# A product of 512 columns for the expert scores, with its halves added by ScalarE and VectorE

## The reference

```
q = x @ w_q                          # 256 x 2048: 8 heads, two halves of 128 each
s = q . sub_keys                     # 128 keys for each head and half
top_s, top_i = top_k(s, 16)          # 16 best keys of each half
best_s, best_c = top_k(sums of pairs, 16)        # 16 of 16 x 16 pairs
expert = i1 * 128 + i2               # one of 16384 experts, 128 per token
gates = softmax(best_s)
h = gelu(x . u_tab[expert])          # exact gelu
y = sum over experts of gates * h * v_tab[expert]
x = LayerNorm(alpha * x + y)
```

## Time and profile before

| | |
|---|---|
| median of three runs | 1952.9 us |
| the profiled execution | 1952.5 us |
| its span | 1950.7 us |
| mean granted TensorE clock | 0.992 |
| busy: TensorE (PE) | 1912.2 us, 98% |
| busy: VectorE (DVE) | 1421.8 us, 73% |
| busy: ScalarE (ACT) | 910.3 us, 47% |
| busy: GpSimd (POOL) | 363.8 us, 19% |
| U tiles of layer 0, first matmul to last | 190.8 to 586.0 us |
| V tiles of layer 0 end | near 966 us |

### The profile page before, as it was taken

One profiled execution on the slowest core, in us unless ns is written; L12 is line 12 of the kernel. 1 busy time (PEld: TensorE's weight loads), 2 busy tenths in 40 slices (PEclk: granted clock), 3 DMA queues, 4 the chain that ended last, 5 costly groups with the idle time before them and its releaser, 6 DMA issues.

```text
span 1950.7 us, 41638 instructions
## 1 busy us (share of the span) xinstructions
PE 1912.2 (98%) x14552; PEld 1713.1 (88%) x14552; DVE 1421.8 (73%) x2405; ACT 910.3 (47%) x1416; POOL 363.8 (19%) x266
## 2 busy tenths in 40 slices
PE   8989999999999999999999899999999999999998
PEld 7779999999998888888787799999999988888886
DVE  7978997577778888544588789975777788884445
ACT  6445454444444444444364454544444444444443
POOL 0000000000004444444300000000000044444443
PEclk9999999999999999999999999999999999999999
DMA  6244556554545455655452445565454545547553
GB/s 228 90 150 154 181 175 202 164 169 154 169 158 166 162 161 172 236 184 192 142 173 91 161 143 183 173 204 168 155 169 155 171 154 170 163 161 245 185 191 109
DMA packets 90502, 328.44 MB, mean 168 GB/s; under 512 B 10049, under 2 KB 10561, under 8 KB 90177
## 3 DMA queue, kind: packets, MB, share of 16 engines
q1 hardware_dynamic: 87264, 316.71, 50.0%
q10 hardware_dynamic: 3168, 10.89, 1.6%
HBM read 324.41 MB, written 3.15 MB: 168 GB/s over the span
## 4 chain that ended last, share of the span: by engine, by line
PE 91%; DVE 4%; issue 3%; ACT 1%; DMA 1%; DVEq 0%; POOL 0%; SPq 0%; ACTq 0%; POOLq 0%
PE bank L1140 15%; PE bank L1141 14%; PE bank L1142 14%; PE bank L1155 13%; PE bank L1157 13%; PE bank L1156 13%; PE bank L1377 5%; DVE conv_acc L734 1%; PE bank L1222 1%; PE bank L1347 1%; DVE lo L665 0%; DVE residual L699 0%; DVE small L689 0%; DMA raw<-in_stream 0%; PE bank L1266 0%
## 5 line engine op out<-in xcount | busy, mean ns | idle before, releaser
L665 DVE TENSOR_TENSOR lo<-raw,hi 128x1024 fp32r<-128x1024 f32 x600 | 766.1, 1279 | 262.5 <-ACT hi L402 260.7
L402 ACT ACTIVATE hi<-raw 128x1024 fp32r<-128x1024 f32 x600 | 634.1, 1059 | 465.9 <-PE bank L1157 439.9
L1140 PE MATMUL bank<-xt,hi 128*128 128x256 f32 x2432 | 696.9, 287 | 5.1 <-DVE xt L671 4.7
L1142 PE MATMUL bank<-xt,lo 128*128 128x256 f32 x2432 | 687.0, 282 | 0.0
L1141 PE MATMUL bank<-xt,hi 128*128 128x256 f32 x2432 | 686.9, 282 | 0.0
L380 POOL TENSOR_TENSOR w_split<-h,w_split 128x256 fp32r<-128x256 f32 x256 | 362.4, 1416 | 1569.4 <-ACT w_split L603 1179.3
L1140 PEld LDWEIGHTS bank<-xt,hi 128*128 128x128 f32 x2432 | 460.9, 190 | 9.7 <-DVE xt L671 4.3
L1141 PEld LDWEIGHTS bank<-xt,hi 128*128 128x128 f32 x2432 | 461.0, 190 | 0.0
L1142 PEld LDWEIGHTS bank<-xt,lo 128*128 128x128 f32 x2432 | 460.6, 189 | 0.0
L1155 PE MATMUL bank<-hi,w_split 128*128 128x512 f32 x1024 | 409.4, 400 | 0.6 <-POOL w_split L380 0.6
L1157 PE MATMUL bank<-hi,w_split 128*128 128x512 f32 x1024 | 404.4, 395 | 0.0
(11 more groups left out here) (165 smaller groups left out, 1070.4 us busy)
## 6 DMA issues: line engine op xcount, KB each, us to landing
raw<-in_stream SPq DMA_DIRECT2D x600, 512.0 KB, 3.7
ln_g<-in_ln_p ACTq DMA_DIRECT2D x4, 512.0 KB, 7.7
ln_b<-in_ln_p ACTq DMA_DIRECT2D x4, 512.0 KB, 9.7
keys_sb<-in_keys_t ACTq DMA_DIRECT2D x2, 1024.0 KB, 5.2
x_kept<-x ACTq DMA_DIRECT2D x4, 512.0 KB, 5.8
x<-x_kept ACTq DMA_DIRECT2D x4, 512.0 KB, 7.4
x<-in_x SPq DMA_DIRECT2D x2, 512.0 KB, 4.9
result<-x SPq DMA_DIRECT2D x4, 256.0 KB, 2.0
```

The costliest lines, as they stand in the source:

```text
L402: nc.scalar.activation(hi[:, j, :], raw[:, j, :], ACT.Copy).then_inc(*hi_done.one)
L665: vec.tensor_tensor(lo[:, j, :], raw[:, j, :], hi[:, j, :].bitcast(f32), ALU.subtract).then_inc(*lo_done[j].one)
L1140: mm(dst, w_hi, xt[:, k, 0, :], start=k == 0, stop=False)
L1142: last = mm(dst, w_lo, xt[:, k, 0, :], start=False, stop=k == KC - 1)
```

## The change

- A U tile is no longer computed by tile_by_x (which stays for AG and WQ tiles). The high weight is multiplied by both parts of x in one product of 512 columns: the lower half of the bank gets high by high, the upper half gets high by low. The low weight times the high x goes to the lower half in a product of 256 columns, as before. So there are 16 matmuls per tile instead of 24.
- ScalarE copies the upper half to h (u_half). VectorE adds the lower half of the bank to it, in place in h (add_halves, signal u_added). ScalarE then takes the gelu in place in h, three tiles late (GELU_LAG = 3).
- TensorE's reuse of a bank waits for u_added in place of gelu_done.
- On VectorE, each low part n from tile U4 on is followed at once by the add of tile n - 4 (ADD_LAG = 4), also between the steps of the choice. The lists of low parts are the same.
- The exponential of the gates moves on ScalarE from turn 8 to turn 9, and the transposes of the chosen keys from turn 11 to turn 13.
- The first gate_block of each segment waits for the last adds and gelus, which are written out ahead of it.

```diff
-EXP_TURN, CHOSEN_TURN = 8, 11
+EXP_TURN, CHOSEN_TURN = 9, 13
+ADD_LAG, GELU_LAG = RING, RING - 1
...
-        gelu_done = signal("gelu_done", NK, primed=RING)
+        u_half, u_added = signal("u_half_kept", NK), signal("u_added", NK, primed=RING)
+        gelu_done = signal("gelu_done", NK)
...
+                def gelu(i, j):
+                    act.wait_ge(*u_added(layer, RING * i + (j + 1)))
+                    act.sem_inc(act_held, 1)
+                    nc.scalar.activation(u_block(i, j), u_block(i, j), ACT.Gelu)\
+                      .then_inc(*gelu_done.one)
...
                         act.wait_ge(*tile_used(layer, RING * i + (U0 + j + 1)))
-                        nc.scalar.activation(h[:, ds(i * (RING * SEQ) + j * SEQ, SEQ)],
-                                             ring_banks[j][:, 0:SEQ], ACT.Gelu)\
-                          .then_inc(*gelu_done.one)
+                        nc.scalar.activation(u_block(i, j), ring_banks[j][:, SEQ:2 * SEQ],
+                                             ACT.Copy).then_inc(*u_half.one)
+                        if not first or j >= GELU_LAG:
+                            gelu(i, j - GELU_LAG)
...
+                def add_halves(i, j):
+                    dve.wait_ge(*u_half(layer, RING * i + (j + 1)))
+                    here = h[:, ds(i * (RING * SEQ) + j * SEQ, SEQ)]
+                    vec.tensor_tensor(here, ring_banks[j][:, 0:SEQ], here, ALU.add)\
+                       .then_inc(*u_added.one)
...
                     for n in range(made[0], made[0] + count):
                         rest(0, n)
+                        if n - ADD_LAG >= U0:
+                            add_halves((n - ADD_LAG - U0) // RING, n % RING)
...
                         for j in range(GROUP_TILES):
-                            rest(i + first_tile // RING, GROUP_TILES * k + j + LO_LEAD)
+                            if seg == 0:
+                                u_rest(i + G_TURN, GROUP_TILES * k + j, first and k == 0)
+                            else:
+                                rest(i + V0 // RING, GROUP_TILES * k + j + LO_LEAD)
...
+                for j in range(LO_LEAD, RING):
+                    add_halves(G_TURN - 1, j)
                 dve.wait_ge(*gelu_done(layer, SEG))
...
                 def u_tile(i, j, last_of_x=False):
                     pe.wait_ge(*lo_done[j](layer, i + (U0 // RING + 1)))
-
-                    pe.wait_ge(*gelu_done(layer, RING * i + (j - RING + 1)))
-                    tile_by_x(j, ring_banks[j][:, 0:SEQ], last_of_x)
+                    pe.wait_ge(*u_added(layer, RING * i + (j - RING + 1)))
+                    dst = ring_banks[j]
+                    for k in range(KC):
+                        w_hi, w_lo = hi[:, j, k * P:(k + 1) * P], lo[:, j, k * P:(k + 1) * P]
+                        both = xt[:, k, :, :].rearrange("p s t -> p (s t)")
+                        if k:
+                            mm(dst[:, 0:SEQ], w_lo, xt[:, k, 0, :], start=False, stop=False)
+                        last = mm(dst[:, :], w_hi, both, start=k == 0, stop=k == KC - 1)
+                        if k == 0:
+                            last = mm(dst[:, 0:SEQ], w_lo, xt[:, k, 0, :], start=False, stop=False)
```

More of the change, by code:

```diff
@@ L317, in build @@
         out_done = signal("out_done", 1, 16)
+        act_held = ctx.enter_context(nc.semaphore("act_held"))
         pe_held = ctx.enter_context(nc.semaphore("pe_held"))
@@ L391, in _ @@
             act.wait_ge(*consts_made(0, 1))
-            for _ in range(RING):
-                act.sem_inc(gelu_done.sem, 1)
             with act.Fori(0, DEPTH) as layer:
@@ L564, in _, with u_block, u_turn @@
                 nc.scalar.preload_act_table(ACT.Gelu)
-                def u_turn(i, before_last=None, after_first=None):
+                def u_block(i, j):
+                    return h[:, ds(i * (RING * SEQ) + j * SEQ, SEQ)]
+                def gelu(i, j):
[3 more added lines that the diff above has]
+                      .then_inc(*gelu_done.one)
+                def u_turn(i, before_last=None, after_first=None, first=False):
                     for j in range(RING):
@@ L573, in u_turn, with last_gelus @@
                         act.wait_ge(*tile_used(layer, RING * i + (U0 + j + 1)))
-                        nc.scalar.activation(h[:, ds(i * (RING * SEQ) + j * SEQ, SEQ)],
-                                             ring_banks[j][:, 0:SEQ], ACT.Gelu)\
-                          .then_inc(*gelu_done.one)
-                u_turn(0, after_first=lambda: score_group(SCORE_GROUPS - 1))
+                        nc.scalar.activation(u_block(i, j), ring_banks[j][:, SEQ:2 * SEQ],
+                                             ACT.Copy).then_inc(*u_half.one)
+                        if not first or j >= GELU_LAG:
+                            gelu(i, j - GELU_LAG)
+                def last_gelus(i):
+                    for j in range(RING - GELU_LAG, RING):
+                        gelu(i, j)
+                u_turn(0, after_first=lambda: score_group(SCORE_GROUPS - 1), first=True)
                 with act.Fori(1, EXP_TURN) as i:
@@ L586, in _ @@
                     u_turn(i)
+                last_gelus(G_TURN - 1)
                 act.wait_ge(*tables(layer, TT))
-                with act.Fori(G_TURN, LAST) as i:
+                u_turn(G_TURN, first=True)
+                with act.Fori(G_TURN + 1, LAST) as i:
                     u_turn(i)
@@ L606, in _ @@
                 u_turn(LAST, first_w_heads)
+                last_gelus(LAST)
                 def v_turn(i):
@@ L651, in _ @@
                 dve.sem_inc(w_done.sem, 1)
+            for _ in range(RING):
+                dve.sem_inc(u_added.sem, 1)
             vec.tensor_copy(ident_b[:, :], ident[:, :]).then_inc(*masks_made.one)
@@ L1031, in _, with u_rest @@
                 dve.sem_inc(dve_held, 1)
+                def u_rest(i, j, alone=False):
+                    rest(i + U0 // RING, j + LO_LEAD)
+                    if not alone:
+                        add_halves(i + (j + LO_LEAD) // RING - ADD_LAG // RING,
+                                   (j + LO_LEAD) % RING)
                 def u_rests(i):
                     for j in range(RING):
-                        rest(i + U0 // RING, j + LO_LEAD)
+                        u_rest(i, j)
                 with dve.Fori(CHOSEN_TURN + 1, G_TURN) as i:
@@ L1072, in gate_block, with gate_turn @@
                                       ALU.mult).then_inc(*w_done.one)
-                def gate_turn(seg, i, first_tile, following):
+                def gate_turn(seg, i, following, first=False):
                     for k in range(TURN_GROUPS):
@@ L1087, in _ @@
                 gated(0, 0, 0)
+                for j in range(LO_LEAD, RING):
+                    add_halves(G_TURN - 1, j)
                 dve.wait_ge(*gelu_done(layer, SEG))
                 dve.sem_inc(dve_held, 1)
-                with dve.Fori(0, G_TURN - 1) as i:
-                    gate_turn(0, i, U0 + NK // 2, (0, i + 1, 0))
-                gate_turn(0, G_TURN - 1, U0 + NK // 2, (1, 0, 0))
+                gate_turn(0, 0, (0, 1, 0), first=True)
+                with dve.Fori(1, G_TURN - 1) as i:
+                    gate_turn(0, i, (0, i + 1, 0))
+                gate_turn(0, G_TURN - 1, (1, 0, 0))
+                for j in range(LO_LEAD, RING):
+                    add_halves(LAST, j)
                 dve.wait_ge(*gelu_done(layer, NK))
@@ L1097, in _ @@
                 with dve.Fori(0, G_TURN - 1) as i:
-                    gate_turn(1, i, V0, (1, i + 1, 0))
-                gate_turn(1, G_TURN - 1, V0, None)
+                    gate_turn(1, i, (1, i + 1, 0))
+                gate_turn(1, G_TURN - 1, None)
                 with dve.Fori(G_TURN, LAST) as i:
@@ L1130, in transpose_x, with tile_by_x @@
                                 last.then_inc(*xt_ps.one)
-                def tile_by_x(slot, dst, last_of_x=False, xt_before=None):
+                def tile_by_x(slot, dst, xt_before=None):
                     for k in range(KC):
@@ L1142, in tile_by_x @@
                         last = mm(dst, w_lo, xt[:, k, 0, :], start=False, stop=k == KC - 1)
-                        if last_of_x and k == WHI_LEAD - 1:
-                            last.then_inc(*xt_used.one)
                     last.then_inc(*tile_used.one)
@@ L1364, in u_tile @@
                     pe.wait_ge(*lo_done[j](layer, i + (U0 // RING + 1)))
-                    pe.wait_ge(*gelu_done(layer, RING * i + (j - RING + 1)))
-                    tile_by_x(j, ring_banks[j][:, 0:SEQ], last_of_x)
+                    pe.wait_ge(*u_added(layer, RING * i + (j - RING + 1)))
[8 more added lines that the diff above has]
+                            last = mm(dst[:, 0:SEQ], w_lo, xt[:, k, 0, :], start=False, stop=False)
+                        if last_of_x and k == WHI_LEAD - 1:
+                            last.then_inc(*xt_used.one)
+                    last.then_inc(*tile_used.one)
```

(2 more changed lines are left out.)

## The result

The changed kernel takes 1971.1 us (median of 4 runs, 1970.3 to 1972.1), the kernel before 1954.6 us (median of 4, 1952.9 to 1958.3). The ratio is 1.008, with a 95% interval of 1.0068 to 1.0093: 0.8% slower, where 1970.0 was forecast. The profiled execution has a span of 1970.2 us, against 1950.7.

The account below looks back on a forecast made before the run. VectorE was taken to bound U4 to U39 of each layer. Over two layers, +24.5 us for the adds and -7.0 us for shorter tiles made +17.5 on 1952.5 us, so 1970.0 us, with a range of 1962 to 1979.

Parts of the forecast that it names:

- The bound: U4 to U39 of each layer: VectorE, busy 101.2 of 102.1 us, already sets the pace and TensorE waits for it.
- The loss: U4 to U39: 36 adds of 0.34 us on a full VectorE lengthen the stretch by 12.2 us per layer.
- The gain: U39 to the end of U127: 89 tiles each 0.039 us shorter on TensorE, -3.5 us per layer.
- The places without a cost: After the choice, beside the gate matrices and where they or the V tiles begin: adds are hidden, at zero cost.
- the same chain stands, and the same answer holds: Start of the V tiles: the wait for copy, add and last gelus is hidden as at the first gate matrices.
- the same chain at the first gate matrices: After U63: copy, add and last gelus end about 0.75 us later than the matmuls awaited before, hidden by 0.7 us.
- The turns: Exponential at turn 9, transposes at 13: they prevent a TensorE wait at the transposes and are priced at zero.

Follow-up runs that it names:

- e2: The kernel before with only the U tiles' matmuls changed (8 of 512, 8 of 256 columns), old gelu, no additions: 1945.7 us, ratio 0.9957.
- e1: The changed kernel without VectorE's additions for U0 to U53, all waits and signals kept: 1950.7 us, ratio 0.998.
- e6: The changed kernel with a second addition of the same form ahead of each of the first 38 additions: 1997.7 us, ratio 1.0216.
- e8: The changed kernel with the additions between the steps of the choice over only 128 of 256 columns: 1967.6 us.
- e7: e5 with the last four U tiles of each layer (U124 to U127) in the old form too: 1947.4 us, ratio 0.9961.
- e4: The changed kernel with the exponential and the transposes of the chosen keys back at turns 8 and 11: 1971.9 us, ratio 1.0085.
- e5b: The same kernel as e5, measured again beside e7 on one chip: 1952.0 us, ratio 0.9981.
- e5: The changed kernel with the old form for U0 to U43, the new from U44, exponential and transposes at turns 8 and 11: 1950.9 us, ratio 0.9979.
- e3: The changed kernel with 24 matmuls of 256 columns per U tile as before, copies, additions and lagged gelus kept: 1981.9 us, ratio 1.0138.

## Why the prediction was right

*The bound.* VectorE was said to set the pace from U4 to U39 in the kernel before, against a busy TensorE of 100%. e2 shows it (a third of the matmuls gone, 102.03 us all the same), and so the 73% of the page's mean was the wrong number to go by.

*The loss.* Forecast 36 x 0.34 = 12.2 us per layer, measured 11.66. The add costs 0.324 and not 0.34; e1, e6 and e8 give it by removal, by doubling and by half. It is the sum's largest term and was 5% too large. (The add behind U4's low part, 0.2 us per layer ahead of U4, was not in the sum.)

*The gain.* Forecast 0.039 us per tile, measured 0.044: 2.803 us per tile and 6.407 us per two tiles with gate matrices, against 2.809 and 6.41. For U39 to U127 this made -3.7 us per layer; -3.5 was forecast. 8 matmuls fewer (and their weight loads), at equal columns, are worth 5.5 ns each here. The Trainium skill's 6 cycles per matmul ("TensorE: Matmul & The Clock Gate", back-to-back issue gap), which it gives for the gap of an isolated matmul, would make 2.5 ns; the measurement decides for the larger one.

*The places without a cost.* It held after the choice, beside the gate matrices and where they begin (U66 starts 2.4 us after its low part). It failed at the start of the V tiles: "the same chain stands, and the same answer holds" was not worked out. This is the timeline of VectorE there in the changed kernel, with the operation of GpSimd and the gate matrices that matter.

```profile
597.10 0.69 DVE L1110 TENSOR_TENSOR h<-bank,h 128x512 f32 x1 [1.30 <-ACT h L575]
597.71 0.95 DVE L1085 TENSOR_TENSOR onehots<-key_blocks,i_t 128x1536 bf16<-128x1536 bf16 x1
598.58 1.77 DVE L688 TENSOR_TENSOR lo<-raw,hi 128x1024 fp32r<-128x1024 f32 x1
600.26 1.49 DVE L1095 TENSOR_TENSOR gated_a<-onehots,gate_part 128x1536 bf16<-128x1536 bf16 x1
...
600.18 0.76 POOL L383 TENSOR_TENSOR w_split<-h,w_split 128x256 fp32r<-128x256 f32 x1 [0.92 <-ACT w_split L616]
...
601.81 0.87 PE L1432 MATMUL bank<-gated_a,onehots 128*128 128x64 bf16 x24 [0.41 <-DVE gated_a L1095]
```

And the same operations in the kernel before:

```profile
587.00 0.69 DVE L1071 TENSOR_TENSOR h<-bank,h 128x512 f32 x1 [1.99 <-PE bank L1377]
587.61 0.95 DVE L1046 TENSOR_TENSOR onehots<-key_blocks,i_t 128x1536 bf16<-128x1536 bf16 x1
588.47 1.76 DVE L665 TENSOR_TENSOR lo<-raw,hi 128x1024 fp32r<-128x1024 f32 x1
590.16 0.94 DVE L1056 TENSOR_TENSOR gated_a<-onehots,gate_part 128x1536 bf16<-128x1536 bf16 x1
...
592.28 0.88 PE L1377 MATMUL bank<-gated_a,onehots 128*128 128x64 bf16 x24
```

Before, the factors are ready at 591.10, 1.18 us ahead of the gate matrices. After the change the gate block waits for the last gelu (line 575) and starts 5.13 us behind the start of U127 (591.97) instead of 3.96 (U127 at 583.04): 1.17 us later, where the prediction put 0.75 for the same chain at the first gate matrices. By these rows that alone would just have been covered. But so shifted, the gated factors run beside GpSimd's split of h and take 1.49 us instead of 0.94; TensorE waits 0.41 us and starts its gate matrices 9.84 us behind the start of U127 instead of 9.24. In all eleven traces this operation takes 1.48 to 1.50 us in just the 16 places where GpSimd's split overlaps it (by some 0.67 us), one in each layer of the eight that have this chain, and at most 0.96 us in the others, which none overlaps. In e7 the last U tiles are in the old form, the block doesn't wait for a gelu, and the same operations stand as before (U127 starts at 578.50):

```profile
582.46 0.69 DVE L1131 TENSOR_TENSOR h<-bank,h 128x512 f32 x1 [1.99 <-PE bank L1462]
...
585.62 0.94 DVE L1116 TENSOR_TENSOR gated_a<-onehots,gate_part 128x1536 bf16<-128x1536 bf16 x1
...
587.74 0.88 PE L1462 MATMUL bank<-gated_a,onehots 128*128 128x64 bf16 x24
```

That was 1.2 us in two layers, priced at zero; e7 shows that the chain causes it, and how it divides between the later block and the slower factors is read from these rows, not tested. *The turns* were priced at zero, and e4 confirms it; but the reason given, that they prevent a wait of TensorE, was wrong: at turn 11 there is none.

Over two layers the errors are 1.2 us too much for the loss, 0.4 too little for the gain and 1.2 left out at the V tiles; they nearly cancel. The forecast difference of 17.5 us stands against 17.1 in the four stretches, 16.5 between the medians and 19.5 between the spans of the two profiled executions. That the total lies 1.1 us from the forecast is in part luck; the terms are right to about 1.2 us each over two layers.

## What to carry to other kernels

Before giving an engine more work, look at its busy share in every stretch. Here VectorE was at 73% as a mean and at 99% for 102 us per layer, and 36 operations of 0.32 us in those 102 us cost more than 8 matmuls less in each of the 89 tiles behind them gave back. An engine that shows 100% busy is not yet the bound: compare its time per tile in the stretch with its time per tile elsewhere. And a gain that is real can be kept by using the new form only where the engine that pays has room: e7 takes the same change to 0.4% under before.

## What the runs showed of the hardware that was not expected

Runs of one kernel spread by 2 to 9 us (e5b 1946.0 to 1955.1), as much as the effects of e5 and e7. Part of it is TensorE's granted clock in the attention stage of each layer. The window of 94 to 104 us, in the kernel before and in e3, whose work up to U0 is the same:

```profile
94.00:104.00 10.00, 9.81 (x56) 7.04 (x57) 7.05 (x22) 8.36 (x25) 0.00 (x0) 1.00 0.44 145
```

```profile
94.00:104.00 10.00, 10.00 (x30) 7.02 (x30) 5.86 (x17) 5.68 (x15) 0.00 (x0) 0.50 0.18 65
```

The clock is at 2.4 GHz (1.00) in the one and at 1.2 GHz (0.50) in the other, for the same work; 56 matmuls fall in the one window and 30 in the other. Just ahead of it TensorE was idle for 1.9 us, waiting for ScalarE's copy of v, and it is so in all eleven traces, in both layers. What follows is not the same, even for one kernel (e5 and e5b). From the end of this idle time to U0 of layer 0:

| low clock behind the idle time, layer 0 | profiled execution of | us to U0 |
|---|---|---|
| none | before, after, e2, e5b, e7 | 96.5 to 96.7 |
| 3.4 us | e4, e5 | 98.1 to 98.2 |
| 10.2 us | e1, e3, e6, e8 | 101.2 to 101.4 |

So 10.2 us at the low clock cost 4.6 us here, and 3.4 us cost 1.5. In layer 1 the stretch at the low clock lasts 3.4 us in most of the traces, none in e5b, 6.8 us in e8 and 10.2 us in e1, and the way to U0 goes with it: 97.0 us in e5b, 98.1 to 98.6 in most, 100.3 in e8, 101.3 in e1. The executions of e1 agree: those of 1947 us have a mean granted clock of 0.992, those of 1954 to 1955 us one of 0.987. Which execution gets the low clock is not told apart by anything I could see in the traces before that point. It is not the whole spread either: the idle time itself ends between 93.2 us (e7) and 96.7 us (e8).

The second is the add's price: 1.02 ns per column and 0.06 us per instruction on a full VectorE, 0.324 us in all, where its row in the profile says 0.42 us. For an engine that is the bound it is the distance from start to start that counts.

The third is what GpSimd does to a neighbour. The operation on 1536 bf16 elements that makes the gated factors takes at most 0.96 us where GpSimd is idle, and 1.48 to 1.50 us where an operation of GpSimd overlaps it by 0.67 us. A low part beside GpSimd takes up to 1.77 us (598.58 in the rows above) where it else takes 1.22. A shift in time can so make an operation longer that the change doesn't touch.
